# The up projection of a decoder block in half-height matmuls: two tiles at a time on the upper and lower 64 rows of the array

## The reference

```python
h = rms_norm(x, norm_mlp[l])
x = x + jnp.square(jax.nn.relu(h @ w_up[l])) @ w_down[l]      # w_up 1024 x 4096, w_down 4096 x 1024
```

## Time and profile before

| what | value |
|---|---|
| time, median of 3 runs (lowest, highest) | 770.01 us (769.87, 770.87) |
| the profiled execution: own time, span of its instructions | 770.08 us, 768.2 us |
| granted TensorE clock over the span | 0.999 |
| PE busy, share of the span | 760.7 us, 99% |
| PEld / DVE / POOL / ACT busy | 81% / 67% / 60% / 44% |
| up projection: matmuls | 768 (3 lines x 256) |
| share of the ended-last chain on PE | 95% |

### The profile page before, as it was taken

How to read it: one execution, slowest core, us unless ns; L and a number is a source line. 1 busy time by engine, 2 the same in 40 slices (tenths; PEclk the granted TensorE clock), 3 DMA queues, 4 the chain that set the end, 5 groups by cost and what they waited for, 6 DMA issues and landing times.

```text
span 768.2 us, 11763 instructions
## 1 busy us (share of the span) xinstructions
PE 760.7 (99%) x4546; PEld 624.4 (81%) x4546; DVE 511.6 (67%) x707; ACT 335.7 (44%) x595; POOL 461.4 (60%) x277
## 2 busy tenths in 40 slices
PE   8999999999999999999999999999999999999997
PEld 7788777988777788878888888888888888888886
DVE  5796488966578546644457766725787277927798
ACT  6200672456421646635121355544553456335641
POOL 5566554677456666665665793456645592658365
PEclk9999999999999999999999999999999999999999
DMA  8244322233522100016232540424123420542002
GB/s 291 84 127 175 111 65 78 83 110 110 185 89 83 56 28 29 28 56 192 86 106 96 189 155 27 165 83 137 56 97 123 137 83 16 181 133 86 25 1 109
DMA packets 24137, 78.16 MB, mean 102 GB/s; under 512 B 2787, under 2 KB 3563, under 8 KB 24084
## 3 DMA queue, kind: packets, MB, share of 16 engines
q1 hardware_dynamic: 21116, 71.10, 27.3%
q10 hardware_dynamic: 2968, 6.34, 2.5%
HBM read 75.31 MB, written 4.21 MB: 104 GB/s over the span
## 4 chain that ended last, share of the span: by engine, by line
PE 95%; DVE 2%; POOL 1%; DMA 1%; ACT 0%; issue 0%; SPq 0%; DVEq 0%; POOLq 0%; ACTq 0%
PE bank L572 20%; PE bank L574 20%; PE bank L573 20%; PE bank L1053 6%; PE bank L1054 6%; PE bank L1052 6%; PE bank L919 3%; PE bank L952 3%; PE bank L964 2%; PE bank L666 2%; PE bank L667 1%; PE bank L668 1%; DVE fin L2002 1%; PE bank L715 1%; DMA x<-in_xT 1%; DVE hlo L1531 1%
## 5 line engine op out<-in xcount | busy, mean ns | idle before, releaser
L449 POOL TENSOR_TENSOR wsp<-wraw,wsp 128x1024 fp32r<-128x1024 f32 x60 | 146.8, 2447 | 5.0
L572 PE MATMUL bank<-hhi,wsp 128*128 128x512 f32 x352 | 140.8, 400 | 1.3 <-DVE hlo L1531 0.7
L447 POOL TENSOR_SCALAR wsp<-wraw 128x1024 fp32r<-128x1024 f32 x60 | 64.5, 1074 | 121.7 <-PE bank L574 108.9
L574 PE MATMUL bank<-hhi,wsp 128*128 128x512 f32 x352 | 137.4, 390 | 0.0
L573 PE MATMUL bank<-hlo,wsp 128*128 128x512 f32 x352 | 137.1, 389 | 0.0
L533 POOL TENSOR_TENSOR wsp<-wraw,wsp 128x1024 fp32r<-128x1024 f32 x24 | 67.7, 2828 | 82.2 <-ACT wsp L1457 81.9
L513 POOL TENSOR_TENSOR wsp<-wraw,wsp 128x1024 fp32r<-128x1024 f32 x32 | 77.9, 2438 | 43.5 <-ACT wsp L1457 43.2
L572 PE MATMUL bank<-ghi,wsp 128*128 128x512 f32 x256 | 99.7, 389 | 0.0
L574 PE MATMUL bank<-ghi,wsp 128*128 128x512 f32 x256 | 99.6, 389 | 0.0
L573 PE MATMUL bank<-glo,wsp 128*128 128x512 f32 x256 | 99.6, 389 | 0.0
L1052 PE MATMUL bank<-wsp,fhi 128*128 128x512 f32 x224 | 87.5, 391 | 0.0
(11 more groups left out here) (311 smaller groups left out, 1447.7 us busy)
## 6 DMA issues: line engine op xcount, KB each, us to landing
wraw<-in_w SPq DMA_DIRECT2D x126, 512.0 KB, 3.3
bias_skewed<-bias_lines ACTq DMA_DIRECT2D x1, 2048.0 KB
bias<-bias_skewed ACTq DMA_DIRECT2D x1, 2048.0 KB, 8.8
out<-fin SPq DMA_DIRECT2D x8, 256.0 KB, 2.1
x<-in_xT SPq DMA_DIRECT2D x3, 512.0 KB, 6.5
x<-in_xT ACTq DMA_DIRECT2D x3, 512.0 KB, 7.8
x<-in_xT SPq DMA_DIRECT2D x2, 256.0 KB, 4.2
wraw<-in_w SPq DMA_DIRECT2D x4, 128.0 KB, 7.1
```

The costliest lines, as they stand in the source:

```text
L447: pool.tensor_scalar(whi[:, two, :], wraw[:, raw, :], 1.0, 0.0, ALU.mult, ALU.add).then_inc(w_hi, 1)
L449: pool.tensor_tensor(wlo[:, two, :], wraw[:, raw, :], whi[:, two, :].bitcast(F32), ALU.subtract).then_inc(w_split, 1)
L572: pe.matmul(out_, wh, mh, start=first, stop=False)
L574: return pe.matmul(out_, wl, mh, start=False, stop=last)
```

## The change

`up_tile` goes. `up_pair` takes two tiles at a time. In the first half of a pair (`swap` 0) each matmul on the upper 64 rows works for tile `t` and the next one, on the lower 64 rows, for tile `t` + 1; in the second half (`swap` 1) they trade tiles. So each tile gets the upper rows of all `k` from one half and the lower rows from the other. A matmul has half as many rows, and there are twice as many (1536). After each half PE waits for its own last two matmuls (`rows_done`), and after the second half it increments `w_used` twice, once for each tile. The pair waits at its start for the low parts of both tiles, and for both banks in the first quarter.

```diff
+            def half_tile(q, t, k, part, rows, first, last):
+                hi, lo = split_slot(STEPS * q + t)
+                cols = slice(k * P, k * P + P)
+                return pe.matmul(z_bank(t)[:], (hi, hi, lo)[part][rows, cols], (ghi, glo, ghi)[part][rows, k, :],
+                                 start=first and k == 0 and part == 0, stop=last and k == KT - 1 and part == 2,
+                                 skip_group_check=True)
+
+            def up_pair(q, t):
+                pair = PAIRS * q + t // 2
+                pe.wait_ge(up_low, UP_T * q + t + 2)
+                if q == 0 and t == 0:
+                    pe.wait_ge(free[0], (U0 + 1) // 2)
+                    pe.wait_ge(free[1], U0 // 2)
                 if t == 2 and q:
                     pe.wait_ge(b_read, 3 * q)
                 if t in (4, 6):
                     pe.wait_ge(form_low, 4 * (pair - 2) + 4)
+                for swap in range(2):
+                    for k in range(KT):
+                        if q == 0 and t == 0 and swap == 0:
+                            pe.wait_ge(g_lo, k + 1)
+                        for part in range(3):
+                            top = half_tile(q, t + swap, k, part, slice(0, 64), swap == 0, swap == 1)
+                            bottom = half_tile(q, t + 1 - swap, k, part, slice(64, P), swap == 0, swap == 1)
+                    top.then_inc(rows_done, 1)
+                    bottom.then_inc(rows_done, 1)
+                    pe.wait_ge(rows_done, 4 * pair + 2 * swap + 2)
+                pe.sem_inc(w_used, 1)
+                pe.sem_inc(w_used, 1)
...
-                for t in range(UP_T):
-                    up_tile(q, t)
+                for t in range(0, UP_T, 2):
+                    up_pair(q, t)
                     if q == 0 and t == 2:
                         mlp_stat()
```

More of the change, by code:

```diff
@@ L279, in build_block @@
         x_turned, xt_kept = sem("x_turned"), sem("xt_kept")
-        first_half_out = sem("first_half_out")
+        first_half_out, rows_done = sem("first_half_out"), sem("rows_done")
         y_ready, y_out = sem("y_ready"), sem("y_out")
```

## The result

The changed kernel takes 824.34 us (823.08 to 825.40, 3 runs) against 770.01: a ratio of 1.0701, 95% interval 1.0687 to 1.0715. It is 54 us slower; the forecast was 819 in a range of 798 to 842.

What follows compares the result with a forecast made beforehand. The prediction took PE as the bound, busy 760.7 of 768.2 us. Its terms, 0 + 10.3 + 1.6 + 1.0 + 4.0 + 27.6 + 5 = 49.5 us on 770.08, gave 819 us, range 798 to 842.

Steps and rivals of the forecast that it cites:

- slots of the couples: MLP up stages: a pair of half-height matmuls takes one slot of 0.227 us, so 0 us change (-10.2 to 10.2).
- 32 waits and 32 increments: Up stages: PE's 32 waits for itself cost 10.3 us (8 to 14), its w_used increments 1.6 (0 to 3).
- changes of tiling: Entering the 64-row form once a quarter and once behind mlp_stat costs 5 x 0.2 = 1.0 us.
- start of the first quarter: The first pair waits for POOL's low part of tile 1: 4.0 us (3.5 to 4.5).
- stalls in the products, idle time: Each quarter PE waits 6.0 us for t1's second half and 0.9 for form_low: 27.6 us in all (18 to 30).
- the clock: PE's clock falls in the five new stalls of 4 to 6 us; restarts cost 1.0 each, 5 us (0 to 10).
- Side by side for fp32r at 64 rows: Up stages: upper and lower matmuls with split operands run at the same time, as the trace showed for plain f32.
- The bound below: Up stages: a slot might fall from 0.227 to 0.213 us, 10.2 us less over 768 slots.
- the second wait of 0.9: In each quarter's product, PE waits about 0.9 us for form_low of the last pair, after the 6.0 us stall.
- serial halves (993): Rival, up stages: each half takes its own 0.227 us slot, 174 us more, 993 us; chance 6%.
- a hidden end of stage (788): Rival, end of up stages: ACT or DVE come through sooner and the stall stays hidden, 788 us; chance 6%.
- a faster kernel: Rival, up stages: a pair of halves is much shorter than a slot; at 0.150 us it gives 760; chance 3%.

Runs made afterwards that it cites:

- the filler: The changed kernel with 20 matmuls of no use put in front of the wait for the second half of t1 in each quarter: 819.32 us (1.0629).

## Why the prediction was right

The forecast's steps beside what the changed kernel's trace has (span 53.0 us longer):

| step | forecast, us | measured, us |
|---|---|---|
| slots of the couples | 0 (-10 to 10) | 1.2 (768 x 0.0016) |
| 32 waits and 32 increments | 11.9 | 17.1 (16 x 0.35 + 16 x 0.72) |
| changes of tiling | 1.0 | 0.9 |
| start of the first quarter | 4.0 | 3.9 (4.08 between starts, less a slot) |
| stalls in the products, idle time | 27.6 | 20.4 (4 x 5.1) |
| the clock | 5 | 9.5, and 0.5 for free loads behind the stalls |
| sum | 49.5 | 53.5 |

The sum of the measured terms is 0.5 above the difference of the spans; the up stage's beginning came 0.45 us earlier for reasons ahead of it (its last matmul before stands at 432.35, against 432.80).

Every step of the forecast is there, but that the sum came so near is in part luck: the stalls were 7.2 us too large, the waits 5.2 and the clock 4.5 too small, and these errors took each other back. The waits lie at the upper end of their bounds taken together (8 to 14, and 0 to 3 for the increments), and so does the clock (0 to 10).

- *Side by side for fp32r at 64 rows*: right, and shown by its opposite, the two matmuls on the same rows. The bound below (0.213 a slot) was not reached, with 0.228 a couple, and it was read wrongly off: less drain and load, the two rounds took 1.02 - 0.09 - 0.03 = 0.90 us, or 0.45 each, twice the 0.213 of 512 columns and not next to it. (The line issues 8 matmuls and the trace has 16, so each f32 matmul seems to stand there twice.) What that row does show, that the tiles run at the same time, held for fp32r.
- *The waits*: the middle was sized right (0.35 for 0.32). The end of a pair was too small by 0.3: I took 0.05 for an increment behind a drain, and the trace shows 0.15 for each. The same increments cost nothing in the running stream of the kernel before, so it is behind PE's wait for itself that they are paid.
- *The start*: right to 0.2 us.
- *The stall in the products*: the mechanism was right in its order, POOL's second low part ahead of L1965 of the kernel before (L1977 now). The size was off in three small ways. The low part of t1's second half came 8.2 us after the relu of tile 6 rather than 8.6 (685.75 - 677.53). PE came to the product 0.3 after that relu, not 0.1, held by the increments. Together with the free load, which I had left out, this makes the first stall 5.1 and not 6.0. And the second wait of 0.9 did not show, for the slow clock covered it; it came back at 0.67 with the filler.
- *The clock*: right in kind, too small by nearly half. I had let the second wait swallow part of each cold restart, which it did, but in two of the four products the clock was low for 6.8 us and not for 3.4 (the second quarter against the third, above). The rows of before held a single fall and a single return, too few to see that both lengths occur.
- *Rivals*: serial halves (993), a hidden end of stage (788) and a faster kernel all fell. The number for serial halves would have been too low itself, since it took the clock as full.

## What to carry to other kernels

When two units of work are merged, look first at whom they used to release one at a time: here the engines behind the matmuls had one tile's time to work off each tile, and two told of together cost more (34 us) than the new form of the matmul (20 us). A wait of the matrix engine for itself costs the drain, the hop and a free load (0.35 us here), and an increment queued behind it, free elsewhere, costs 0.15. Idle time of the matrix engine of 4 to 5 us had a second price in its clock at all five places here (2.7 us of it at one of four), which falls due behind the stall and can hide another wait.

## What the runs showed of the hardware that was not expected

- With matmuls on the upper 64 rows alone, one after another and PE busy 99% of the time, the granted clock stayed at 0.50 over 80 us in one quarter and fell to 0.50 in mid-stage in the next, for 122 us of the up stage. The mean over the kernel was 0.769 (one run). With couples on both halves it did not fall in the midst of an up stage.
- fp32r matmuls of 64 rows run in couples at 0.228 us for 512 columns, no faster than one of 128 rows (0.227), and their two loads run side by side in 0.19 us.
- After a stall of 5.1 us the clock was low for 3.4 us in some cases and 6.8 in others, in the same kernel and at the same place of a quarter.
